# First-pass loads, latents and rotary keys rearranged in a two-block transformer kernel on one Trainium2 core

## The reference, cut to what matters

```python
h = x @ w_in                      # x: (2048, 1024)
x_q, x_kv, k_rope_raw, gate_a, u_pool, gate_b = split(h, 512, 256, 64, ...)
cos, sin = rope_cos_sin(positions)
q  = (rms_norm(x_q, q_norm_g) @ w_uq)          # 4 heads x (128 + 64)
kv = (rms_norm(x_kv, kv_norm_g) @ w_ukv)       # 4 heads x (128 keys + 128 values)
k_rope = apply_rope(k_rope_raw, cos, sin)      # [t1*cos - t2*sin, t1*sin + t2*cos]
o = softmax(q_nope @ k_nope + q_rope @ k_rope, causal) @ v
```

## Time and profile before

| | |
|---|---|
| median of 3 runs | 3687.98 us (3687.55 to 3689.05) |
| the profiled execution | 3689.07 us, of which the span is 3687.2 us |
| PE busy | 3439.4 us, 93% of the span |
| DVE, ACT, POOL busy | 1931.4, 1348.2 and 548.1 us |
| mean granted PE clock | 0.96 of full speed |
| the first slice of 92 us | PE 0.7 busy, DMA 0.5 busy at 180 GB/s; in the slices behind it PE is at 0.9 |

### The profile page before, as it was taken

How to read it: one execution, slowest core, us unless ns; L and a number is a source line. 1 busy time by engine, 2 the same in 40 slices (tenths; PEclk the granted TensorE clock), 3 DMA queues, 4 the chain that set the end, 5 groups by cost and what they waited for, 6 DMA issues and landing times.

```text
span 3687.2 us, 46244 instructions
## 1 busy us (share of the span) xinstructions
PE 3439.4 (93%) x17264; PEld 1841.9 (50%) x17264; DVE 1931.4 (52%) x4676; ACT 1348.2 (37%) x2565; POOL 548.1 (15%) x1001
## 2 busy tenths in 40 slices
PE   7999999999999999999989989899898898898887
PEld 3344544454455445545555445654555543455563
DVE  3406722672275327434562577825758625868642
ACT  1212312231222113122341465524766514776551
POOL 0001011102100210011121201201352101342000
PEclk9999999999999999989989999899899999998998
DMA  5121013002300220141103111021110031110001
GB/s 180 56 65 67 2 58 122 21 1 74 120 7 14 76 89 2 41 148 63 63 6 117 62 64 42 24 93 68 52 55 1 24 106 57 49 55 1 1 27 66
DMA packets 72062, 206.30 MB, mean 56 GB/s; under 512 B 6392, under 2 KB 7968, under 8 KB 71584
## 3 DMA queue, kind: packets, MB, share of 16 engines
q1 hardware_dynamic: 63504, 187.61, 15.1%
q10 hardware_dynamic: 8336, 15.74, 1.2%
HBM read 185.75 MB, written 17.58 MB: 55 GB/s over the span
## 4 chain that ended last, share of the span: by engine, by line
PE 79%; DVE 10%; ACT 5%; issue 4%; POOL 1%; SPq 0%; DMA 0%; ACTq 0%; DVEq 0%; POOLq 0%
PE bank L1944 43%; PE o_acc L2064 6%; PE bank L2047 6%; PE bank L2292 3%; PE bank L2054 3%; PE bank L2173 3%; PE bank L2205 3%; PE bank L2304 2%; PE o_acc L2318 2%; PE bank L2144 1%; PE bank L1975 1%; DVE tmp L1650 1%; ACT index L1310 1%; PE bank L1981 1%; ACT prob_t L1174 1%
## 5 line engine op out<-in xcount | busy, mean ns | idle before, releaser
L1944 PE MATMUL bank<-group_even,weights 128*128 128x512 f32 x1376 | 605.6, 598 | 18.5 <-DMA weights<-in_w_in_kv 12.7
L1944 PE MATMUL bank<-group_odd,weights 128*128 128x512 f32 x1376 | 607.1, 598 | 6.2 <-ACT tmp L1160 6.2
L1944 PE MATMUL bank<-y_all,weights 128*128 128x512 f32 x1024 | 441.2, 592 | 6.3 <-DVE y_all L1905 6.3
L1944 PEld LDWEIGHTS bank<-group_even,weights 128*128 128x128 f32 x1376 | 261.5, 192 | 338.7 <-issue 338.5
L1944 PEld LDWEIGHTS bank<-group_odd,weights 128*128 128x128 f32 x1376 | 261.7, 192 | 327.9 <-issue 327.5
L1119 ACT ACTIVATE probs<-probs,stat 128x512 f32<-128x512 f32 x256 | 181.7, 711 | 424.0 <-DVE stat L1414 424.0
L1944 PEld LDWEIGHTS bank<-y_all,weights 128*128 128x128 f32 x1024 | 194.2, 190 | 250.3 <-issue 243.0
L2064 PEld LDWEIGHTS o_acc<-lat,val 128*128 128x128 f32 x2048 | 245.0, 199 | 44.2 <-issue 40.3
L2064 PE MATMUL o_acc<-lat,val 128*128 128x128 f32 x2048 | 254.6, 285 | 7.7 <-DVE lat L1479 7.4
L2047 PE MATMUL bank<-k_nope,q_nope 128*32 128x512 f32 x2048 | 233.0, 595 | 0.0
L1465 DVE CUSTOM_DVE_ANT_0 probs<-bank,mask 128x512 f32<-128x512 f32 x256 | 161.4, 687 | 102.5 <-PE bank L2054 102.5
(11 more groups left out here) (388 smaller groups left out, 5146.5 us busy)
## 6 DMA issues: line engine op xcount, KB each, us to landing
weights<-in_w_in SPq DMA_DIRECT2D x101, 512.0 KB, 3.5
weights<-in_w_in_q SPq DMA_DIRECT2D x64, 512.0 KB, 3.4
weights<-in_w_out SPq DMA_DIRECT2D x64, 512.0 KB, 3.5
weights<-in_w_i SPq DMA_DIRECT2D x20, 512.0 KB, 3.5
group_even<-in_x_t SPq DMA_DIRECT2D x8, 1024.0 KB, 8.2
group_odd<-in_x_t SPq DMA_DIRECT2D x8, 1024.0 KB, 9.0
group_even<-x_t SPq DMA_DIRECT2D x8, 1024.0 KB, 7.9
group_odd<-x_t SPq DMA_DIRECT2D x8, 1024.0 KB, 7.9
```

Source lines behind the costliest of these rows:

```text
L1944: ins = M(bank(*name)[:], ring[n % SLOTS][:, k * P:(k + 1) * P], rhs[:, k, :], start=(at == 0), stop=(at == chunks - 1))
```

## The change

1. **Loads.** Group 0's x comes as four transfers of 512 KB, each with a semaphore of its own (`x_part`), behind the first weight tile. PE starts the first tile when the first transfer is there and waits for the others as it comes to them. The small vector of gains (`vec`) is loaded behind them with its own semaphore; the other seven constants stay where they were.
2. **Order on ACT and DVE.** ACT waits at the start only for `vec`. In each group it does the latents and the root first and the rotary tables after. DVE does the reciprocal and the scaling first and waits for the tables and rotates after.
3. **Early query tile.** In group 3 PE computes ("xq", 0, 0) where the other groups compute the next kv tile. ACT's waits for its target buffers are adapted.
4. **Rotary key tile.** `project_halves` multiplies blocks of 128 x 64 weights: even chunks sum into partitions 0 to 63, odd ones into 64 to 127. `rotate_keys` adds the two halves on 64 rows, makes the products and writes the result twice.

The diff, cut to its core:

```diff
@@ first_pair_steps / query_tiles
     if g + 1 < G:
         yield ("kv", g + 1, 0)
+    else:
+        yield ("xq", 0, 0)
...
-    yield ("xq", g, 0)
     if g > 0:
+        yield ("xq", g, 0)
         yield ("1mean", g - 1)
@@ SP
-            def load_x(g, src):
+            def load_x(g, src, first=False):
+                if first:
+                    for k in range(0, KC, 2):
+                        sp.dma_start(x_of(g)[:, k:k + 2, :], src[:, k:k + 2, g * TB:(g + 1) * TB]).then_inc(x_part[k // 2], 16)
+                    return
...
-                if name[0] == "kv" and name[2] == 0:
+                if name[0] == "kv" and name[2] == 0 and name[1] > 0:
...
                 sent += 1
+                if sent == 1:
+                    load_x(0, A["x_t"], first=True)
+                    sp.dma_start(vec[:], A["vec"]).then_inc(vec_here, 16)
@@ ACT
-            act.wait_ge(const_here, 16 * 8)
+            act.wait_ge(vec_here, 16)
             act.wait_ge(const_made, 4)
             for g in range(G):
-                rope_tables(g)
...
-                kv_latents(g, range(0 if g == 0 else 1, 2))
+                if g == 0:
+                    kv_latents(0, range(1))
+                kv_latents(g, range(1, 2))
                 root(("kv_sq", g), KVR, 0, (k_normed, g) if g else None)
+                rope_tables(g)
                 if g + 1 < G:
                     kv_latents(g + 1, range(1))
+                else:
+                    latents("xq", 0, range(1), y_of(0), VEC["q_g"], None)
@@ DVE
+            def rotate_keys(g):
+                wait_tile(dve, "krope", g)
+                both = bank("krope", g)
+                low, high = slice(0, ROPE), slice(ROPE, P)
+                step(dve, V.tensor_copy(tmp[low, 0, :], both[high, :]))
+                drains(V.tensor_tensor(tmp[low, 1, :], both[low, :], tmp[low, 0, :], ALU.add), "krope", g)
+                wait_drained(dve, "krope", g)
+                for to in range(2):
+                    of = slice((to ^ 1) * ROPE // 2, ((to ^ 1) + 1) * ROPE // 2)
+                    step(dve, V.tensor_tensor(o_sb[to * ROPE // 2:(to + 1) * ROPE // 2, :], tmp[of, 1, :], sin[of, :], ALU.mult))
+                step(dve, V.tensor_tensor(tmp[low, 0, :], tmp[low, 1, :], cos[low, :], ALU.mult))
+                for rows in (low, high):
+                    step(dve, V.tensor_tensor(k_rope[rows, g * TB:(g + 1) * TB], tmp[low, 0, :], o_sb[low, :], ALU.add))
...
             for g in range(G):
                 rope_args(g, g)
-                dve.wait_ge(rope_made, g + 1)
-                rotate("krope", g)
-                step(dve, V.tensor_tensor(k_rope[:, g * TB:(g + 1) * TB], tmp[:, 0, :], tmp[:, 1, :], ALU.add))
                 wait_drained(dve, "kv_sq", g)
                 step(dve, V.reciprocal(rstd[:], std[:]))
                 kv_lat = lat[:, 2 * (g % 2):2 * (g % 2) + 2, :]
                 V.tensor_tensor(kv_lat, kv_lat, wide(rstd[:], 2), ALU.mult).then_inc(k_normed, 1)
+                dve.wait_ge(rope_made, g + 1)
+                rotate_keys(g)
@@ PE
+            def project_halves(name, rhs, chunks):
+                n = WSLOT[name]
+                pe.wait_ge(w_here[n % SLOTS], 16 * (n // SLOTS + 1))
+                claim(*name)
+                for k in range(chunks):
+                    part = slice((k % 2) * ROPE, (k % 2 + 1) * ROPE)
+                    ins = M(bank(*name)[part, :], ring[n % SLOTS][:, k * P + part.start:k * P + part.stop], rhs[:, k, :],
+                            start=(k < 2), stop=(k >= chunks - 2))
+                ins.then_inc(tile_ready, 1)
...
                 if g == 0:
-                    wait_x(pe, g, 0)
-                    project(("kv", g, 0), x_of(g), KC)
+                    project(("kv", g, 0), x_of(g), KC, parts=True)
                 project(("kv", g, 1), x_of(g), KC)
-                project(("krope", g), x_of(g), KC)
+                project_halves(("krope", g), x_of(g), KC)
...
                     project(("kv", g + 1, 0), x_of(g + 1), KC)
+                else:
+                    wait_x(pe, 0, G // 2)
+                    project(("xq", 0, 0), x_of(0), KC)
```

More of the change, by code:

```diff
@@ L631, in program @@
         const_here = sem("const_here")
+        vec_here = sem("vec_here")
         x_here = [sem(f"x_here{i}") for i in range(2)]
+        x_part = [sem(f"x_part{i}") for i in range(KC // 2)]
         const_made = sem("const_made")
@@ L714, in wait_x @@
         def wait_x(eng, g, before):
-            eng.wait_ge(x_here[g % 2], 32 * (before + 1))
+            eng.wait_ge(x_here[g % 2], 32 * (before + 1 - (g % 2 == 0)))
         def wait_tile(eng, *name):
@@ L808, in _ @@
         def _(sp):
-            first_constants = ((vec[:], A["vec"]), (pos_qi, A["pos_q"]), (pos_k4_i, A["pos_k4"]), (pos_i, A["pos_k"].broadcast_to([P, S])),
+            first_constants = ((pos_qi, A["pos_q"]), (pos_k4_i, A["pos_k4"]), (pos_i, A["pos_k"].broadcast_to([P, S])),
                                (w_ukv, A["w_ukv"]), (ident[:], A["ident"]), (pool_w[:], A["pool_w"]), (pool_cnt[:], A["pool_cnt"]))
-            def load_x(g, src):
+            def load_x(g, src, first=False):
[3 more added lines that the diff above has]
+                    return
                 for k in range(0, KC, 4):
@@ L1042, in latents @@
                         step(act, ins)
-                    if j == 0 and before is not None:
+                    if tag == "xq" and g == 0 and j in (0, 2):
+                        wait_tile(act, "v", G - 2 + j // 2, BG - 1)
+                    elif j == 0 and before is not None:
                         wait_tile(act, *before)
@@ L1088, in _ @@
                 rope_tables(G + g)
-                latents("xq", g, range(4), y_of(g), VEC["q_g"], ("v", G - 1, BG - 1) if g == 0 else ("mix", g - 1, 3))
+                latents("xq", g, range(1 if g == 0 else 0, 4), y_of(g), VEC["q_g"], ("v", G - 1, BG - 1) if g == 0 else ("mix", g - 1, 3))
                 if g > 0:
@@ L1373, in rotate @@
                 wait_drained(dve, *name)
+            def rotate_keys(g):
[11 more added lines that the diff above has]
+                    step(dve, V.tensor_tensor(k_rope[rows, g * TB:(g + 1) * TB], tmp[low, 0, :], o_sb[low, :], ALU.add))
             def wide(ap, n):
                 return ap.unsqueeze(1).broadcast_to([P, n, TB])
-            dve.wait_ge(const_here, 16 * 8)
+            dve.wait_ge(vec_here, 16)
+            dve.wait_ge(const_here, 16 * 7)
             step(dve, V.tensor_copy(pos_k[:], pos_i))
@@ L1933, in claim, with project @@
                     pe.wait_ge(drained[n % RING], n // RING)
-            def project(name, rhs, chunks, heads_made=None):
+            def project(name, rhs, chunks, heads_made=None, parts=False):
                 n = WSLOT[name]
@@ L1941, in project @@
                 for at, k in enumerate(order):
+                    if parts and k % 2 == 0:
+                        pe.wait_ge(x_part[k // 2], 16)
                     if heads_made is not None and k == 0:
@@ L1967, in _ @@
                     project(("kv", g + 1, 0), x_of(g + 1), KC)
+                else:
+                    wait_x(pe, 0, G // 2)
+                    project(("xq", 0, 0), x_of(0), KC)
                 if g == 0:
-                    pe.wait_ge(const_here, 16 * 8)
+                    pe.wait_ge(const_here, 16 * 7)
                 pe.wait_ge(k_normed, g + 1)
@@ L2001, in _ @@
             for g in range(G):
-                wait_x(pe, g, G // 2 + g // 2)
-                project(("xq", g, 0), x_of(g), KC)
                 if g > 0:
+                    wait_x(pe, g, G // 2 + g // 2)
+                    project(("xq", g, 0), x_of(g), KC)
                     mean_of("1", g - 1)
```

## The result

| | before | changed |
|---|---|---|
| median of the first 4 executions | 3687.77 us (3684.73 to 3689.05) | 3648.63 us (3647.13 to 3649.0) |
| ratio, 95% interval | | 0.990 (0.9888 to 0.9912) |
| span of the profiled execution | 3687.2 us | 3647.0 us |
| all executions of this study | 64, mean 3685.1 us (3680.4 to 3689.1) | 12, mean 3649.9 us (3647.1 to 3652.5) |

The forecast was 3658.4 us, with a range from 3654 to 3664. The changed kernel is faster, as forecast, but by 39.1 us in the first four executions where my sum gave 29.6; over all executions of the study it is 35.3 us.

What follows compares the result with a forecast made beforehand. PE was taken to bound the kernel (79% of the chain ending last). Gains 8.0 + 1.4 + 10.3 + 9.9 = 29.6 us took 3689.07 to 3659.5, as a median 3658.4; range 3655 to 3662, with rivals 3654 to 3664.

Steps and rivals of the forecast that it cites:

- Part 1, the start: Group 0: first matmul near 7.4 us, worth nothing by itself; key tiles 10.73 us earlier, net 8.0 after low clock.
- the constants' chain: Group 0: last constant lands at 28.85 us as before, within 1.5; DVE's angles, then scaling, give k_normed at 43.39.
- The wait before the key tiles: Group 0: PE, through at 35.2 us, waits 8.2 us for the scaled latents.
- the low clock behind it: Group 0 key tiles: the clock falls after PE's idle stretch, costing 2.74 us, bounds 1.6 to 3.9.
- Part 2, order: Groups 1 and 2: scaling no longer stands behind the rotation on DVE, gaining 0.69 us each, 1.4 in all.
- The covers I named: Work moved behind the scaling on DVE and ACT costs PE nothing; the smallest slack is 1.2 us, between 5.6 and 6.87.
- Part 3, the early query tile: Group 3: a query tile fills PE's 7.56 us gap before the key tiles and avoids 2.74 of low clock; gain 10.3.
- Part 4, column halves: Rotary key tile: two halves run side by side, 3.57 us for 6.87; gain 9.9 us over groups 1 to 3.
- The rival that weights would be exposed: Rotary tile: each column step waits for its own weights, 4.5 us a tile, total 3661.3; chance 0.06.
- the second rival: Rotary tile: halves run one after the other, tile stays 6.87 us, no gain there, total 3668.3; chance 0.07.
- From 188 us on everything should only stand 30 us earlier.: Everything behind the first pass keeps its length and only shifts about 30 us earlier.
- my upper bounds: Whole forecast: constants 1.5 us, clock 1.1, halves 0.9 and small losses 1, given as reaching 3662.

Runs made afterwards that it cites:

- two_loads: Changed kernel with group 0's x in two 1 MB transfers in front of the first weight tile, as before; 3646.56 us.
- b_dve5: Kernel before with five tiny one-column copies on DVE in the first pass, where DVE idles; 3682.52 us, ratio 0.9991 to before.
- b_dve5_again: Repeat of the kernel before with five tiny DVE copies in the first pass; 3681.25 us, ratio 0.9985 to before.
- no_halves: Changed kernel with the rotary key tile computed at full 128 columns and rotated by the old code, in its new place; 3661.72 us.
- b_pad043: Kernel before with one extra half-width PE matmul (about 0.43 us) in front of second-pass tile gate_a, 0, 1, product overwritten; 3687.15 us.
- b_pad171: Kernel before with two extra full-width PE matmuls (about 1.72 us) in front of second-pass tile gate_a, 0, 1, product overwritten; 3686.75 us.

## Why the prediction was right in the first pass and wrong in the total

**Part 1, the start: right in kind.** I said the early first tile is worth nothing since the constants' chain ends last; two_loads shows it. The wait before the key tiles was 7.33 us (8.2 forecast), the low clock behind it cost 3.07 (2.74). One term was off: I let the constants land at the same time, and they came 1.5 us earlier, at the edge of my bound. That is nearly all of the difference between the 12.3 us gained and the 10.7 forecast. The first matmul came at 6.01 for 7.4, which changed nothing.

**Part 2, order: right.** Undoing it costs 10.4 us, and PE has no wait in groups 1 to 3. The covers I named held.

**Part 3, the early query tile: right.** Group 3 gained 13.4 with the rotary tile's share, for 13.6.

**Part 4, column halves: right.** The rotary tile takes 65.54 to 69.13, 3.59 us for the 3.57 of the sum. The rival that weights would be exposed gave 4.5: by the Trainium skill, TensorE: Matmul & The Clock Gate, "The mechanism", weight loads overlap matmuls only where row groups differ; this tile's halves share all rows and show no such cost, so the measurement decides. The kernel before had shown it already: in its full-width tiles, which share all rows too, a weight load of 0.19 us stands at every 0.43 us and 16 instructions take 6.87. The halves run side by side, and not in turn as the second rival had it.

**The step that failed** is one sentence: "From 188 us on everything should only stand 30 us earlier." The forecast was 29.6; the first four executions of each kernel gave 39.1. The first pass gave 30.4, 0.8 more. The base made 2.9: I took the median of three executions, 3687.98, for a kernel whose 64 executions average 3685.1. The changed kernel's first four lay 1.2 under its mean. What is left, 35.3 - 30.4 = 4.9 us, lies behind the first pass. The stretch behind the query squares was not left as it was: it got shorter, by 4.8 us on the means of three profiles each. That is of the size that nine DVE entries alone (the five copies) bring in the kernel before (4.2). The change moves DVE's later instructions too, by five entries, as a by-product of the new rotation and one more wait.

At the first of the two places all three profiles of the old stream wait 1.85 to 1.87 us, and two of them lose 1.6 us at the low clock. At the second all three wait 1.31, and two lose 3.2. The 13 profiles of b_dve5, b_dve5_again, b_dve16, the changed kernel and its variants with the new rotation wait 1.65 to 1.67 and 1.21 and lose nothing at either place. Two thirds of 1.6 + 3.2 are 3.2 us, my estimate from these rows of what the two places bring out of the 4.8. That the rest comes from positions too is an inference from the sizes. no_halves has one entry more than the kernel before, is 3.5 us slower than its parts explain, and loses 3.2 us at the second place. But its waits do not fit simply: 2.01 us at the first place without a fall, and only 1.23 at the second with one. So at these places the longer waits went with more falls, but the length of the wait alone does not decide.

```profile
2875.53 3.36 PE L2340 MATMUL bank<-kh,qa 64*128 64x512 f32 x6 [1.23 <-DVE o_sb L1934]
```

What stays open: why only about a quarter of the entries at the late positions are late, and why sixteen copies bring 7 us where five bring 4.

**The range** from 3654 to 3664 missed the 3648.6 by 5 us. It held the bounds of the terms, but no term for the code that is not touched. The bare scatter of the kernel before, 3680.4 to 3689.1, was nearly as wide as my whole range of 10 us, and three executions within 1.5 us of each other did not show it. Three smaller slips changed no verdict: my upper bounds add up to 3662.9 and not 3662, the groups should have been 36.84 - 4.0 = 32.8 us apart and not 32.6 (32.97 measured), and 125 us at half clock would have given 3783 and not 3750.

## What to carry to other kernels

Ask of an earlier start first what ends last behind it: here 7 us of earlier matmuls ended in a wait, and the wait's low clock took back part of another gain. Take what feeds the next matmuls (reciprocal, scaling) ahead of all on its engine that only a later stage needs, down to the constants it waits for. And a difference of 0.1 to 0.2% in a kernel with many short waits of PE may come from where instructions lie, not from what they do: add a few idle instructions to the old kernel as a control before explaining it, and count semaphore entries with them. Take more than three executions for the base.

## What was not expected of the hardware

A DVE instruction can come 0.1 to 0.35 us late at fixed places of the instruction stream (0.23 us instead of 0.03 between L1408 and L1409). In all 17 profiles the late ones gather at every 128th entry of DVE, 64 beyond the multiples of 128: 142 of 619 are late there, and 331 of 75133 elsewhere. At two places this lengthened a wait of PE from 1.66 to 1.85 and from 1.21 to 1.31 us, and the granted clock fell behind the longer one in the profile of the kernel before (0.66 and 0.51 over 5 and 6 us). Each place shows the fall in two of the three profiles with that DVE stream (before, b_pad043, b_pad171), and in none of the 13 with the shorter waits. So, where it fell, 0.1 us on DVE went with 1.7 us on PE in the six instructions behind it (3.65 for 1.98), and with 3.2 in all. In the kernel without the halves the clock fell behind a wait of 1.23 us and did not behind one of 2.01.
